# Eight groups of gathered experts computed in the final stage, with one tile put last

## What is computed

```python
def peer(x, w_q, keys1, keys2, u_tab, v_tab):      # 8 heads x top 16 of 16,384 experts
    ...
    idx = ...                                      # 128 experts of each token
    g = softmax(sc)
    act = gelu(einsum('thkd,td->thk', u_tab[idx], xb))
    return einsum('thk,thkd->td', g * act, v_tab[idx])

h = h + peer(rmsnorm(h, norm_ffn), ...)
e = rmsnorm(h, norm_ple)
h = h + sigmoid(e @ w_ple_gate) * (p @ w_ple_proj)
y = rmsnorm(h, norm_final)
```

## Time and profile before

| | us |
|---|---|
| median of 3 runs (lowest, highest) | 4860.73 (4858.03, 4862.85) |
| the profiled execution's own time | 4847.97 |
| its span, first to last instruction | 4846.3 |
| stage `exp`: last mix of TensorE ends | 4647.3 |
| stage `ple`: first load issued; last gate ends | 4654.5; 4815.5 |
| busy over the span: PE, DVE, ACT, POOL | 4326.4, 3032.4, 969.1, 1260.3 |
| DMA in all | 1477.7 MB, mean 305 GB/s |

### The profile page before, as it was taken

One profiled execution on the slowest core, in us unless ns is written; L12 is line 12 of the kernel. 1 busy time (PEld: TensorE's weight loads), 2 busy tenths in 40 slices (PEclk: granted clock), 3 DMA queues, 4 the chain that ended last, 5 costly groups with the idle time before them and its releaser, 6 DMA issues. The chain is left out here.

```text
span 4846.3 us, 48883 instructions
## 1 busy us (share of the span) xinstructions
PE 4326.4 (89%) x16974; PEld 2666.9 (55%) x16974; DVE 3032.4 (63%) x6385; ACT 969.1 (20%) x1863; POOL 1260.3 (26%) x969
## 2 busy tenths in 40 slices
PE   8996686989999987888887988869999999999988
PEld 5554453665555545666663766654545455444534
DVE  1002351458777767989881487766889777877743
ACT  1112221111101104555541122220000000000023
POOL 0000031014444442333320000004444444444410
PEclk9998788999999997878878999989999999999999
DMA  4443496769999988978858777749999999999941
GB/s 166 144 146 103 143 320 280 279 245 422 379 386 391 374 337 279 343 286 308 331 218 322 291 256 258 239 149 417 419 404 410 419 419 419 415 415 412 412 184 58
DMA packets 363495, 1477.73 MB, mean 305 GB/s; under 512 B 38338, under 2 KB 178418, under 8 KB 242706
## 3 DMA queue, kind: packets, MB, share of 16 engines
q0 software_dynamic: 119872, 824.76, 42.4%
q1 hardware_dynamic: 193874, 625.13, 34.8%
q10 hardware_dynamic: 49536, 25.17, 1.7%
HBM read 1369.00 MB, written 115.38 MB: 306 GB/s over the span
## 5 line engine op out<-in xcount | busy, mean ns | idle before, releaser
L2552 POOL DMA_INDIRECT ex_uv<-in_uv,idx x768 | 1169.7, 1523 | 1706.2 <-DVE ex_acc L2609 1512.5
L2593 DVE CUSTOM_DVE_ANT_0 ex_uv<-ex_uv,ex_xp 128x1024 f32<-128x1024 f32 x768 | 912.8, 1222 | 290.6 <-DMA ex_uv<-in_uv,idx 243.4
L2609 DVE SCALAR_TENSOR_TENSOR ex_acc<-ex_uv,ex_wt,ex_acc 128x1024 f32<-128x1024 f32 x768 | 943.5, 1282 | 10.8 <-DVE C L893 3.2
L392 PE MATMUL proj_psum_acc<-proj_w,aT_later 128*128 128x385 f32 x2304 | 748.8, 487 | 7.7 <-DMA proj_w<-in_w_in 7.7
L2807 PE MATMUL exp_psum_dn<-exp_dn_big,exp_dn_gg 128*128 128x512 f32 x1536 | 685.1, 596 | 28.7 <-DVE exp_dn_gg L2763 28.6
L2798 PE MATMUL exp_psum_dn<-exp_dn_xT,exp_dn_big 128*128 128x384 f32 x2048 | 683.2, 487 | 6.9 <-DMA exp_dn_big<-in_ud 6.9
L392 PEld LDWEIGHTS proj_psum_acc<-proj_w,aT_later 128*128 128x128 f32 x2304 | 437.0, 190 | 319.1 <-DMA proj_w<-in_w_in 7.9
L2798 PEld LDWEIGHTS exp_psum_dn<-exp_dn_xT,exp_dn_big 128*128 128x128 f32 x2048 | 390.0, 190 | 306.4 <-issue 69.5
L2807 PEld LDWEIGHTS exp_psum_dn<-exp_dn_big,exp_dn_gg 128*128 128x128 f32 x1536 | 291.0, 191 | 379.1 <-issue 351.8
L301 PE MATMUL proj_psum_acc<-proj_w,aT 128*128 128x385 f32 x1152 | 377.4, 488 | 4.5 <-DMA proj_w<-in_w_in 2.6
L301 PEld LDWEIGHTS proj_psum_acc<-proj_w,aT 128*128 128x128 f32 x1152 | 218.5, 190 | 159.4 <-issue 5.1
(11 more groups left out here) (460 smaller groups left out, 4241.7 us busy)
## 6 DMA issues: line engine op xcount, KB each, us to landing
proj_w<-in_w_in SPq DMA_DIRECT2D x48, 1540.0 KB, 10.4
rt_w<-in_w_q SPq DMA_DIRECT2D x36, 2048.0 KB, 8.4
exp_dn_big<-in_ud SPq DMA_DIRECT2D x128, 512.0 KB
exp_dn_big<-in_vd SPq DMA_DIRECT2D x128, 512.0 KB
scratch_z<-proj_zs SPq DMA_DIRECT2D x216, 192.5 KB, 2.0
rt_w<-in_w_br_m SPq DMA_DIRECT2D x18, 2048.0 KB, 9.0
rt_w<-in_w_br_f SPq DMA_DIRECT2D x18, 2048.0 KB, 8.9
rt_w<-in_w_out SPq DMA_DIRECT2D x18, 2048.0 KB, 8.0
```

The costliest lines, as they stand in the source:

```text
L392: mm = pe.matmul(acc[j % SLOTS][:, 0:CW], aT[:, k, t * P:(t + 1) * P], w[:, u % U, k, :], start=(k == 0), stop=(k == KD - 1))
L2552: pool.indirect_dma_start(self.uv[:, slot, :], None, self.uv_tab, bass.IndirectOffsetOnAxis(ap=self.idx[:, at:at + 1], axis=0)).then_inc(s ...
L2593: dve.tensor_tensor_reduce(self.uv[:, slot, 0:D], self.uv[:, slot, 0:D], self.xp[:], 1.0, 0.0, ALU.mult, ALU.add, self.dot[:, g % 2, j:j + ...
L2609: dve.scalar_tensor_tensor(out=self.acc[:, j % 2, :], in0=self.uv[:, slot, D:2 * D], scalar=self.wt[:, g % 2, j:j + 1], in1=self.acc[:, j ...
```

## The change

`TAIL = 8`: the stage `exp` handles 88 of the 96 gathered groups, and its weighings are spread evenly over these 88 groups. The other 8 groups (of tile 5) are computed in `ple`: VectorE and ScalarE work them off in 12 pieces of 6 units, two pieces for each of the first six tiles, one between `front(i + 1)` and `back(i)`, one behind `back(i)`. The first two of these groups are fetched in `exp`, the other six by GpSimd in `ple`. Tile 5 goes last, behind tiles 6, 7 and 8, and its load waits until its finished rows are stored. The buffers of `Experts` stay allocated through `ple`.

```diff
+TAIL = 8
 # stage_experts
-        GROUPS, UNITS = ex.GROUPS, ex.UNITS
-        ROUND = GROUPS // NBLK
-        assert ROUND * NBLK == GROUPS
+        GROUPS, UNITS = ex.GROUPS - TAIL, ex.UNITS
-        after = {ROUND * UNITS * (q + 1) // BLK - 1: q for q in range(BLK)}
+        after = {GROUPS * UNITS * (c + 1) // CH - 1: c for c in range(CH)}
 # gpsimd
-                if g + ex.AHEAD < GROUPS:
-                    ex.fetch(pool, g + ex.AHEAD)
-            ex.rows_end(pool, GROUPS)
+                ex.fetch(pool, g + ex.AHEAD)
 # vector
-            ex.dve_close(dve, GROUPS)
-def stage_ple(nc, K, g_cols, w_gate, w_proj, gain_row, pT, T, t0, nt):
+def stage_ple(nc, K, g_cols, w_gate, w_proj, gain_row, pT, T, tiles, ex):
+        nt = len(tiles)
+        HOSTS = 6
+        g0 = ex.GROUPS - TAIL
+        hosted = lambda i, half: ex.units(g0, ex.GROUPS, 2 * i + half, 2 * HOSTS) if i < HOSTS else ()
+        ends = lambda i: [g for half in range(2) for g, unit in hosted(i, half) if unit == ex.UNITS - 1]
-        rows = lambda i: slice((t0 + i) * P, (t0 + i + 1) * P)
+        rows = lambda i: slice(tiles[i] * P, (tiles[i] + 1) * P)
 # sync
-            for i in range(2, nt):
+            for i in range(2, nt - 1):
                 load(i)
+            sp.wait_ge(ex.stored, ex.nt * 16)
+            load(nt - 1)
 # gpsimd
             for i in range(nt):
+                for g in ends(i):
+                    if g + ex.AHEAD < ex.GROUPS:
+                        ex.fetch(pool, g + ex.AHEAD)
+                if i == HOSTS - 1:
+                    ex.rows_end(pool, ex.GROUPS)
                 pool.wait_ge(y_set, i + 1)
 # scalar (vector alike, with dve_unit)
                 if i + 1 < nt:
                     front(i + 1)
+                for g, unit in hosted(i, 0):
+                    ex.act_unit(act, g, unit)
                 back(i)
+                for g, unit in hosted(i, 1):
+                    ex.act_unit(act, g, unit)
 # vector only
+                if i == HOSTS - 1:
+                    ex.dve_close(dve, ex.GROUPS)
 # trunk_kernel
-        stage_ple(..., T, 0, NT)
+            stage_ple(..., T, [0, 1, 2, 3, 4, 6, 7, 8, 5], ex)
```

More of the change, by code:

```diff
@@ L2875, in _ @@
                     ex.dve_unit(dve, g, unit)
-                    b, at = divmod(g, ROUND)
-                    if at * UNITS + unit in after:
-                        c = b * BLK + after[at * UNITS + unit]
+                    if g * UNITS + unit in after:
+                        c = after[g * UNITS + unit]
                         dn.dve_weigh(dve, c)
@@ L2893, in _ @@
                             dn.act_gelu(act, c)
-                    if at * UNITS + unit in after:
-                        c = b * BLK + after[at * UNITS + unit] + AHEAD
+                    if g * UNITS + unit in after:
+                        c = after[g * UNITS + unit] + AHEAD
                         if c < CH:
@@ L2900, in _ @@
             dn.act_out(act)
-def stage_ple(nc, K, g_cols, w_gate, w_proj, gain_row, pT, T, t0, nt):
-    with Stage(nc, f"ple{t0}") as st:
+def stage_ple(nc, K, g_cols, w_gate, w_proj, gain_row, pT, T, tiles, ex):
+    with Stage(nc, "ple") as st:
+        nt = len(tiles)
[3 more added lines that the diff above has]
+        ends = lambda i: [g for half in range(2) for g, unit in hosted(i, half) if unit == ex.UNITS - 1]
         wg, wp = st.sb("wg", [P, KD, D]), st.sb("wp", [P, 2, D])
@@ L3053, in _ @@
                     front(i + 1)
+                for g, unit in hosted(i, 0):
+                    ex.dve_unit(dve, g, unit)
                 back(i)
+                for g, unit in hosted(i, 1):
+                    ex.dve_unit(dve, g, unit)
+                if i == HOSTS - 1:
+                    ex.dve_close(dve, ex.GROUPS)
 def trunk_kernel(nc, A, O):
@@ L3120, in trunk_kernel @@
             stage_experts(nc, K, ex, idx, gate, A["ud"], A["vd"], T, sc_3, NT - DENSE - 1)
-        stage_ple(nc, K, A["norm_ple"], A["w_ple_gate"], A["w_ple_proj"], A["norm_final"], A["pT"], T, 0, NT)
+            stage_ple(nc, K, A["norm_ple"], A["w_ple_gate"], A["w_ple_proj"], A["norm_final"], A["pT"], T,
+                      [0, 1, 2, 3, 4, 6, 7, 8, 5], ex)
 _OUTS = dict(y=(TOK, D), fox_k=(TOK, W_F), fox_v=(TOK, W_F), fox_lf=(TOK, H_F),
```

## The result

| | before | changed |
|---|---|---|
| median of 19 runs, us | 4861.17 | 4869.99 |
| lowest, highest | 4852.70, 4871.79 | 4861.61, 4881.00 |
| ratio (95% interval) | | 1.0018 (1.0010 to 1.0025) |
| span of the profiled execution | 4846.3 | 4865.8 |
| `exp`: start of the first mix to end of the last | 1342.2 | 1305.0 |

The changed kernel is slower by 8.8 us, 0.18%, with an interval clear of zero. `exp` gave 37.1 us, the boundary took 0.8 and `ple` 45.8; together +9.5. The two spans differ by more, 19.5 us, because the first mix began at 3305.1 in one profile and at 3315.1 in the other, in code that is the same in both.

A forecast was written before the change was run, and what follows sets the result against it. TensorE was taken to bound `ple`, and TensorE and DMA both to be at their limits in `exp`. 45 us paid in `ple` plus 1 at the boundary less 29 won in `exp` gave +17: 4877 us, range 4856 to 4894.

The forecast's parts named there:

- 29 us won: In `exp`, TensorE's waits for weighings vanish but for 3 us, and two slow mixes with them; between 0 and 38.
- the two dips: In `exp`, two mixes of 7.08 instead of 5.39 us, the clock having dipped behind a wait; 1.7 us each, expected to vanish.
- DMA bytes as the bound of `exp`: In `exp`, gathers hold the stage back; DMA need per chunk falls from 10.48 to 9.86 us, under the chunk's 10.31.
- a DMA share under 1.0: Sign expected in the changed profile of `exp`, where the share had been 1.01 at 412 GB/s.
- The boundary: Between `exp` and `ple`, gathers still moving delay the dense stores and gate weights; 1 us, between 0 and 5.
- the 45 taken: In `ple`, the whole cost of the hosted groups: 45 us, between 36 and 57.
- 35.5 + 1.2 + 3.8: In `ple`: six hosted cycles of 23.96 against 18.04 us, the close of tile 5, and late sigmoids and roots from table loads.
- the 4.5 for the clock: In `ple`, TensorE idles 5 to 6 us per hosted cycle, then runs slow; 4.5 us, between 0 and 12.
- rival (d): In `ple`, each exposed table switch also waits for ScalarE to drain; +22, 4883 us; chance 0.06.
- (a): In `ple`, hosted work fits VectorE's idle time, so `ple` pays 6 us; sum -22, 4839 us; chance 0.08.
- (b): In `exp`, the 12.8 us between median and profile may be gather waits that vanish too; +4, 4865 us; chance 0.14.
- (c): In `exp`, landing time or the even spread keeps the 28.6 us of waits; +46, 4907 us; chance 0.10.

The follow-up runs named there:

- with 96 groups: Kernel before, all 96 groups in `exp`, every twelfth gather fetching 128 floats in place of 2048 (7.8% fewer gathered bytes); `exp` took 1306.3 us.
- two groups placed early: Changed kernel with only two groups moved, both in `ple` between first eviction and second norm; median 4841.84 us, ratio 0.9964 to the kernel before.
- Four groups: Changed kernel moving 4 groups, not 8: ratio 0.9978 to before in its order; 0.9929 with two before the second norm, two behind the norm of tile i + 2.
- the placed version of eight groups: Changed kernel, two groups between first eviction and second norm, six behind the norm of tile i + 2, three row buffers; 4827.08 us, ratio 0.9923 to before.
- the even spread alone: Kernel before with all 96 groups kept in `exp` and only the weighings spread evenly as in the changed kernel; `exp` took 1343.2 us.

## Why the prediction was right

It said 4877 and slower, and 4870 was measured; the net of +17 us became +8.8 in the medians and +9.5 in the stages. The mechanism held part by part: `exp` won by bytes, `ple` lost by VectorE's order. One term was mis-sized, and one agreed partly by luck.

**The term that was off: "29 us won" in `exp`.** It measured 37.1, at the very top of the 0 to 38 that the undisturbed pace allowed. Two things were left out of the 29. One is the 3 us kept back for waits around the choice of experts; these went with the bytes, but for 1.4 us with 96 groups and 0.2 with 88. The other is what remained of the 37.9 us of excess behind the 28.6 of waits and the two dips, 5.9 us, put down to "slow clock early in the stage and loop overhead". The rows do not bear that out. The stage keeps the undisturbed pace until its first wait:

```profile
3310.26 5.32 PE L2798 MATMUL exp_psum_dn<-exp_dn_xT,exp_dn_big 128*128 128x384 f32 x16
...
3607.09 5.39 PE L2807 MATMUL exp_psum_dn<-exp_dn_big,exp_dn_gg 128*128 128x512 f32 x12 [2.83 <-DVE exp_dn_gg L2763]
```

From the first mix at 3305.11 to this one are 301.98 us: 29 pairs of 10.31 are 298.99, the wait is 2.83, and 0.16 is left. So there is no slow clock early on, and the rest belongs to the waits. A score and a mix are 5.32 and 5.31 us long, yet the pair takes 10.31, so each group of matmuls overlaps the next by 0.16 us; where TensorE waits, that overlap is lost, and the mix behind the wait is 5.39 us long. An estimate from these rows: 23 waits x 0.16 = 3.7 us, waits 28.6 - 0.2 = 28.4, and the mixes 685.1 - 679.8 = 5.3 (3.4 of it the two dips), together 37.4 for the 37.1 measured. The same sum for two groups placed early is 12.1 + 4.7 + 12 x 0.16 = 18.7 for 18.9. By this estimate a wait of TensorE costs some 0.24 us more than its length in the trace, even where the clock stays up.

**DMA bytes as the bound of `exp`: right**, and now shown against both others, spacing and VectorE's work. The DMA need per chunk of 9.86 us against 10.31 left enough room. The sign named for it, a DMA share under 1.0, came only barely, at 0.99; the wait for weighings is the clearer sign. Four groups show the same: VectorE still waits some 160 us for rows there, and TensorE 1.2 us or less for weighings.

**The boundary: right.** 0.8 us for the 1 taken, inside 0 to 5; with four or two groups it was 1.7 to 3.7.

**`ple`: 45.8 us for the 45 taken, in part by luck.** The six hosted cycles came to 150.0 us (4664.84 to 4814.84) against 6 x 18.04 = 108.2, so 41.8; by its parts the prediction had 35.5 + 1.2 + 3.8 = 40.5, and the clock on top. A cycle was priced at 23.96 us bare, 24.9 with a late sigmoid, and measured 24.25 to 25.13, with 26.33 for the sixth, which holds the close and a slow transpose. Slow transposes were in two of these cycles, not four. Outside them three things came to 4.1 us. The first gate was 1.1 us longer, which the same code does by itself. The cycle behind the hosted ones was 1.0 longer, with a projection of 4.61 us at a mean clock of 0.78 in it, 3.60 before. And the stretch behind the last eviction was 2.0 longer, which no term had: VectorE, ScalarE and the last store keep their distances there, and the store lands 2.9 us after its issue in both kernels, but GpSimd's drain behind it takes 2.83 us in place of 0.78. So the 4.5 for the clock were a little over 3 at most, and the drain filled what they left over.

**The table loads: the rows, not the rule.** The prediction had named the Trainium skill (ScalarE: Activation LUTs, What ACT_TABLE_LOAD costs), which adds a drain of some 1.38 us to each switch. In the changed kernel the Gelu ended at about 4670.89, the load ran from 4670.90, and the sigmoid began at 4672.19:

```profile
4670.68 0.21 ACT L2637 ACTIVATE ex_act<-ex_dot 128x4 f32<-128x4 f32 x1 [17.52 <-DVE ex_dot L2594]
4670.90 1.28 ACT L2975 ACT_TABLE_LOAD   x1
4672.19 1.02 ACT L2975 ACTIVATE ple_sg<-ple_psum_g 128x1024 f32<-128x1024 f32 x1
```

A switch costs the 1.28 us of the load and nothing else that the rows show, so rival (d) did not come.

**The rivals.** (a), the cover that holds, did not happen in the change's order, but its idea was sound: the placed version of eight groups, with 9 units in a cycle in place of 12, has a cycle of 18.2 us, where 12 units had been put at 18.8. What stood against it was named rightly, the norm behind the second piece; that the load of `h` stood right behind that, ready to take its place, was not seen. (b), that the 12.8 us between median and profile were gather waits, is not borne out: the profiled execution of before simply began `exp` early, and over 19 runs its median was 4861. (c), no gain in `exp`, is refuted by the changed kernel itself, and its second half by the even spread alone, with its 28.8 us of waits.

## What to carry to other kernels

When a stage is at two limits at once, move only as much as brings the saturated one under the other: four groups gave all but 1.4 us of what eight gave. When waits are to go, count with each of them the overlap that it breaks. Where moved work is to hide in an in-order engine's idle time, idle microseconds are not enough; it must stand behind every instruction that starts the next round's chain, and ahead only of the one that waits. And when a wait is taken away and nothing changes, look for the next load in line before giving up the idea.

## What was not expected of the hardware

The clock did not follow the length of the gap alone. In `exp` before, the mix behind a wait of 2.33 us took 7.08 us at a granted clock of 0.76, and the one behind a wait of 3.37 us took 5.39 at 1.00; behind waits of 1.98 and 2.83 us they took 7.08 and 5.39. A 512 KB load that lands in 3.3 us on quiet queues took up to 8.2 us beside four gathers of 1 MB, on another queue. GpSimd's drain at the end of `ple` took 0.78 us in the kernel before, 1.53 in both kernels with 8 gathers in that stage, and 2.83 in every kernel with 24, two-buffer or three-buffer, whatever the placement; that the gathers are the cause is not shown. And the same code ahead of `exp` ended anywhere between 3305 and 3329 us over the thirteen profiles. Most of that is in the attention stage, 724 to 744 us long, where the mean granted clock was 0.75 to 0.80 of full speed.
